# A two-block transformer kernel: the second block's attentions by pairs of heads

## The reference, cut to what matters

```python
for layer in range(2):
    u = rms_norm_2(h, norm_g[layer]) * (1 + scale) + shift
    uc = rms_norm_2(hc, norm_g[layer]) * (1 + scale_c) + shift_c
    y, yc = ab_mixer(u, uc, ...) if layer == 0 else c_mixer(u, uc, ...)
    h = h + gate * y            # hc likewise, but not after the last layer
return rms_norm_2(h, final_g)
```

## Time and profile before

| what | us |
|---|---|
| median of 3 runs | 1394.5 |
| lowest and highest | 1389.78, 1398.46 |
| the profiled execution | 1398.49 |
| its span, first to last instruction | 1396.7 |
| PE, DVE, ACT, POOL busy in it | 1267.5, 480.2, 430.7, 213.6 |
| mean granted TensorE clock | 0.963 |

### The profile page before, as it was taken

How to read it: one execution, slowest core, us unless ns; L and a number is a source line. 1 busy time by engine, 2 the same in 40 slices (tenths; PEclk the granted TensorE clock), 3 DMA queues, 4 the chain that set the end, 5 groups by cost and what they waited for, 6 DMA issues and landing times.

```text
span 1396.7 us, 17822 instructions
## 1 busy us (share of the span) xinstructions
PE 1267.5 (91%) x6740; PEld 805.5 (58%) x6740; DVE 480.2 (34%) x1128; ACT 430.7 (31%) x874; POOL 213.6 (15%) x374
## 2 busy tenths in 40 slices
PE   7997999798999999998989999989959899998996
PEld 6875665557533233334344233258848686987985
DVE  3564233443310002122222021133345435356544
ACT  4543333323220001133231001023325343545662
POOL 3004364100010000012010000014302123000320
PEclk9998887899999999999999999999979999999999
DMA  9546387343479999999999999965411203664200
GB/s 365 183 146 224 98 295 241 121 151 118 155 278 409 409 409 409 381 410 409 409 405 407 406 407 398 409 241 180 141 45 46 76 18 107 208 189 145 60 16 31
DMA packets 97037, 333.64 MB, mean 239 GB/s; under 512 B 10416, under 2 KB 10672, under 8 KB 96816
## 3 DMA queue, kind: packets, MB, share of 16 engines
q1 hardware_dynamic: 96944, 332.41, 64.4%
HBM read 331.32 MB, written 1.05 MB: 238 GB/s over the span
## 4 chain that ended last, share of the span: by engine, by line
PE 69%; DMA 16%; DVE 7%; ACT 3%; issue 2%; SPq 1%; POOL 1%; DVEq 0%; POOLq 0%; ACTq 0%
PE ps L453 23%; PE ps L505 8%; DMA w<-in_w_gate 7%; PE ps L1601 6%; DMA w<-in_w_up 6%; PE ps L2142 5%; PE ps L618 5%; PE ps L2185 3%; DMA w<-in_w_down 3%; PE ps L629 3%; PE ps L758 2%; PE ps L537 2%; PE ps L1168 2%; PE ps L1620 2%; PE ps L2161 1%
## 5 line engine op out<-in xcount | busy, mean ns | idle before, releaser
L2142 PE MATMUL ps<-w,vT 128*32 128x512 f32 x1024 | 196.0, 601 | 14.8 <-DMA w<-in_w_gate 8.0
L437 ACT ACTIVATE ab<-w 128x1024 fp32r<-128x1024 f32 (+2 forms) x117 | 121.9, 1048 | 209.4 <-PE ps L453 185.6
L447 DVE TENSOR_TENSOR ab<-w,ab 128x1024 fp32r<-128x1024 f32 (+2 forms) x96 | 117.9, 1234 | 187.7 <-ACT ab L437 187.6
L453 PE MATMUL ps<-ab,UA 128*128 128x512 f32 (+1 forms) x416 | 127.2, 387 | 6.2 <-DVE UB L1207 5.0
L2142 PEld LDWEIGHTS ps<-w,vT 128*32 128x32 f32 x1024 | 37.8, 108 | 152.9 <-issue 64.2
L453 PE MATMUL ps<-ab,uA 128*128 128x512 f32 x320 | 107.7, 419 | 10.7 <-POOL ab L447 4.2
L1601 PE MATMUL ps<-w,Uc 128*128 128x512 f32 (+1 forms) x224 | 102.8, 606 | 1.8 <-DVE Uc L1744 1.8
L453 PEld LDWEIGHTS ps<-ab,UA 128*128 128x128 f32 x416 | 77.7, 188 | 21.6 <-issue 5.3
L2185 PE MATMUL ps<-w,bT 128*32 128x512 f32 x512 | 78.8, 598 | 9.6 <-ACT bT L2238 5.5
L453 PE MATMUL ps<-ab,UB 128*128 128x512 f32 (+1 forms) x208 | 80.4, 386 | 0.0
L453 PEld LDWEIGHTS ps<-ab,uA 128*128 128x128 f32 x320 | 63.5, 202 | 27.5 <-POOL ab L447 4.7
(11 more groups left out here) (493 smaller groups left out, 2023.7 us busy)
## 6 DMA issues: line engine op xcount, KB each, us to landing
w<-in_w_gate SPq DMA_DIRECT2D x128, 512.0 KB, 10.9
w<-in_w_up SPq DMA_DIRECT2D x128, 512.0 KB, 11.7
w<-in_w_down SPq DMA_DIRECT2D x128, 512.0 KB, 11.8
w<-in_w_ada SPq DMA_DIRECT2D x48, 512.0 KB, 6.6
w<-in_w_c SPq DMA_DIRECT2D x48, 512.0 KB, 4.6
w<-in_w_m SPq DMA_DIRECT2D x16, 512.0 KB, 4.8
w<-in_ab_out_w SPq DMA_DIRECT2D x16, 512.0 KB, 7.9
w<-in_w_out SPq DMA_DIRECT2D x8, 512.0 KB, 5.8
```

What stands on the lines that cost most here:

```text
L437: e.activation(sp.a(j), w.v, ACT.Copy).then_inc(sp.whole, 1)
L447: e.tensor_tensor(sp.b(j), w.v, sp.a(j).bitcast(F32), ALU.subtract).then_inc(sp.parts[j % NAB], 1)
L453: ins = e.matmul(out_, l[x], r[y], start=start and n == 0, stop=stop and n == 2)
L2142: ins = e.matmul(t.ps[o, :], ve[:, p % 2, 2 * c + k, o], w.v[:, k, :], start=c + k == 0, stop=c + k == 4)
```

## The change

- WIN, LAT and NEAR become `Pairs`: two neighbouring heads and one query block at a time, 8, 8 and 16 of them. Scores of head 0 use rows 0 to 63 of PE, of head 1 rows 64 to 127, alternating (`halves`; LAT has 96 rows and does not); nothing is zeroed. Queries are scaled by minus 0.125 (or minus 96 to the -0.5), masks have the other sign, and DVE takes the minimum of mask plus scores over all 512 keys in one operation. The output product has the values as stationary operand, 64 columns for each head, so that it comes turned, [features, 128 queries]; two more products spread the reciprocals over it. DVE multiplies both into ZT, which is laid out turned. Transposes follow one step after the scores, outputs two.
- za, zb, c6 and c7 are made turned (`pe_linT`); bo and co are read in the row order "(k p)". The 16 transposes go; ACT and POOL or DVE split ZT in four parts, c = 0 to 3, some of them during the attention, and `pe_out_lin` waits part by part.
- The bias is built by POOL, per pair, into Bm, one pair ahead.
- Norms: the rows are scaled by ACT (row 1) and DVE (row 0) and transposed. For norm1 the mean square comes from the rows times gain before the first block's final norm is applied to h; that norm is moved behind norm1. The gain's row is made in the context's work, ahead of c5.
- The rotations come behind zb.3's split, ACT's splits of bo0 behind WIN; context c3 is run in two halves around the first transposes.

```diff
-        ZO = h[:, 2:4, :]
+        ZT = h[:, 2:4, :].rearrange("p i n -> p (i n)").rearrange("p (k t) -> p k t", k=8)
...
+        def pe_pairs(e, at, need=()):
+            for s, v in need:
+                e.wait_ge(s, v)
+            turned = {}
+            for step in range(at.n + 2):
+                if step < at.n:
+                    pr = at.pairs[step]
+                    ts = [bank.take(ALL, at.tag + "_s") for _ in range(2)]
+                    for t in ts:
+                        free(e, t)
+                    order = [(x, hp) for x in range(len(pr["k"])) for hp in range(2)]
+                    if not at.halves:
+                        order.sort(key=lambda o: o[1])
+                    for x, hp in order:
+                        c, n, k = pr["k"][x]
+                        ins = e.matmul(ts[hp].ps[:, c:c + n], pr["q"][hp], k[hp], start=True, stop=True)
+                        if x == len(pr["k"]) - 1:
+                            ins.then_inc(ts[hp].full, 1)
+                yield
+                p = step - 1
+                if 0 <= p < at.n:
+                    turned[p] = []
+                    for hp in range(2):
+                        t = bank.take(ALL, at.tag + "_t")
+                        free(e, t)
+                        e.wait_ge(*at.prob(2 * p + hp))
+                        for c in range(4):
+                            ins = e.transpose(t.ps[:, c * 128:c * 128 + 128], bP[:, (2 * p + hp) % 3, c * 128:c * 128 + 128], ident)
+                        ins.then_inc(t.full, 1)
+                        turned[p].append(t)
+                yield
+                p = step - 2
+                if p >= 0:
+                    pr, t, m = at.pairs[p], bank.take(ALL, at.tag + "_o"), st[:, p % 4, :]
+                    free(e, t)
+                    e.wait_ge(pair_rec, at.rec0 + p + 1)
+                    for hp in range(2):
+                        o = slice(64 * hp, 64 * hp + 64)
+                        e.matmul(t.ps[o, 128:256], m[:, 4 + hp:5 + hp].to_broadcast([128, 64]), ident, start=True, stop=True)
+                    for x in turned.pop(p):
+                        e.wait_ge(x.evac, x.n)
+                    for c in range(4):
+                        for hp in range(2):
+                            o = slice(64 * hp, 64 * hp + 64)
+                            ins = e.matmul(t.ps[o, 0:128], pr["v"][c][hp], bT[:, (2 * p + hp) % 3, c * 128:c * 128 + 128], start=c == 0, stop=c == 3)
+                    ins.then_inc(t.full, 1)
+                yield
+
+        def dve_pairs(e, at, ready=None):
+            for step in range(at.n + 3):
+                p = step - 3
+                if p >= 0:
+                    t, z = bank[at.tag + "_o"][p], at.pairs[p]["z"]
+                    e.wait_ge(t.full, t.n)
+                    chain(e.tensor_tensor(z, t.ps[:, 128:256], z, ALU.mult))
+                    e.tensor_tensor(z, t.ps[:, 0:128], z, ALU.mult).then_inc(t.evac, 1)
+                yield
+                if step < at.n:
+                    pr, m = at.pairs[step], st[:, step % 4, :]
+                    if ready:
+                        ready(step)
+                    for hp in range(2):
+                        u = 2 * step + hp
+                        t = bank[at.tag + "_s"][u]
+                        e.wait_ge(t.full, t.n)
+                        if at.masked:
+                            if u >= 2:
+                                e.wait_ge(*at.prob(u - 2))
+                            e.tensor_tensor_reduce(bS[:, hp, :], t.ps[:, :], pr["mask"][hp], 1.0, pr["nsink"][hp] if at.sink else 3e38,
+                                                   ALU.add, ALU.min, m[:, hp:hp + 1]).then_inc(t.evac, 1)
+                        else:
+                            e.tensor_reduce(m[:, hp:hp + 1], t.ps[:, :], X, ALU.min).then_inc(pair_top, 1)
+                yield
+                yield
+
+        def act_pairs(e, at, more=None):
+
+            for step in range(at.n + 1):
+                if step < at.n:
+                    m = st[:, step % 4, :]
+                    for hp in range(2):
+                        u = 2 * step + hp
+                        t = bank[at.tag + "_s"][u]
+                        e.wait_ge(*at.top(u))
+                        if u >= 3:
+                            g = bank[at.tag + "_t"][u - 3]
+                            e.wait_ge(g.full, g.n)
+                        src = bS[:, hp, :] if at.masked else t.ps[:, :]
+                        ins = e.activation(bP[:, u % 3, :], src, ACT.Exp, bias=m[:, hp:hp + 1], scale=-1.0, accum_out=m[:, 2 + hp:3 + hp])
+                        ins.then_inc(pair_prob if at.masked else t.evac, 1)
+                if step > 0:
+                    for hp in range(2):
+                        u = 2 * step - 2 + hp
+                        t = bank[at.tag + "_t"][u]
+                        if u >= 3:
+                            g = bank[at.tag + "_o"][(u - 3) // 2]
+                            e.wait_ge(g.full, g.n)
+                        e.wait_ge(t.full, t.n)
+                        e.activation(bT[:, u % 3, :], t.ps[:, :], ACT.Copy).then_inc(t.evac, 1)
+                if at.sink and step < at.n:
+                    e.wait_ge(sink_away, step + 1)
+                    e.activation(m[:, 6:8], m[:, 6:8], ACT.Exp).then_inc(sink_exp, 1)
+                if more:
+                    more(step)
+
+        def pool_pairs(e, at, before_=None):
+            for step in range(at.n):
+                m = st[:, step % 4, :]
+                if before_:
+                    before_(step)
+                if at.sink:
+                    e.wait_ge(*at.top(2 * step))
+                    e.wait_ge(*at.top(2 * step + 1))
+                    e.tensor_tensor(m[:, 6:8], m[:, 0:2], at.pairs[step]["sink"], ALU.add).then_inc(sink_away, 1)
+                e.wait_ge(*at.prob(2 * step))
+                e.wait_ge(*at.prob(2 * step + 1))
+                if at.sink:
+                    e.wait_ge(sink_exp, step + 1)
+                    G_.did(e.tensor_tensor(m[:, 2:4], m[:, 2:4], m[:, 6:8], ALU.add))
+                    G_.after()
+                e.tensor_tensor(m[:, 4:6], m[:, 2:4], C("minus").to_broadcast([128, 2]), ALU.pow).then_inc(pair_rec, 1)
+
+
+        o_upper, o_lower, o_lower_v = sem("o_upper"), sem("o_lower"), sem("o_lower_v")
...
+        def out_lower(e, zT, c, n, done):
+
+            e.wait_ge(o_upper, n)
+            e.tensor_tensor(UB[:, 2 * c:2 * c + 2, :], zT[:, 2 * c:2 * c + 2, :], UA[:, 2 * c:2 * c + 2, :].bitcast(F32), ALU.subtract).then_inc(done, 1)
...
+        def pe_rows_to_T(e, name, n):
+
+            for i in range(2):
+                pe_to_T(e, name, lambda k: scaled_rows[i].rearrange("p (d k) -> p k d", k=8)[:, k, :], 8, ALL,
+                        (diag_ready, 2 + n) if i == 0 else (rows_act, n))
...
-            pe_row_bcast(e, "grown", lambda k: S("gfin")[:, k:k + 1], ALL)
-            some(later, 3)
-            for i in range(2):
-                pe_norm(e, "norm1", i, diag(i), (diag_ready, 3 + i), ALL)
-            some(later, 1)
+            some(later, 2)
+            pe_rows_to_T(e, "norm1", 1)
+            some(later, 2)
...
-            pe_lin(e, S2, "za", UA, UB, 512, range(2), (1, 3))
-            pe_lin(e, S2, "zb", UA, UB, 512, range(2), (1, 3))
-            some(later, 4)
-            for i in range(2):
+            pe_linT(e, S2, "za", UA, UB, (1, 3))
+            pe_linT(e, S2, "zb", UA, UB, (1, 3))
+            for i in range(2):
+                some(later, 2)
                 pe_to_T(e, "qaT", lambda k: qa[:, i, k * 128:(k + 1) * 128], 4, ALL, (kd_ready2, i + 1))
                 pe_to_T(e, "kaT", lambda k: kd[:, k, :, :].rearrange("p a r -> p (a r)"), 2, ALL)
             for i in range(2):
                 pe_to_T(e, "cqT", lambda k: cq[:, i, 0:384].rearrange("p (d k) -> p k d", k=3)[:, k, :], 3, ALL)
                 pe_to_T(e, "ckT", lambda k: ck[:, i, :].rearrange("p (d k) -> p k d", k=2)[:, k, :], 2, ALL)
-            beside(pe_attend(e, WIN, ALL, [(kaT_zero, 2), emptied("kaT")] + [emptied("qaT", i) for i in range(2)]), pe_queries(e))
+            beside(pe_pairs(e, WIN, [emptied("kaT")] + [emptied("qaT", i) for i in range(2)]), pe_queries(e))
...
-            for _ in pe_attend(e, LAT, ALL, []):
+            for _ in pe_pairs(e, LAT):
                 pass
-            e.wait_ge(*emptied("lat_o"))
-            for i in range(2):
-                pe_to_T(e, "mT", lambda k: ZO[:, i, :].rearrange("p (d k) -> p k d", k=8)[:, k, :], 8, ALL)
-            all_emptied(e, "mT")
-            for c in range(2):
-                pe_lin(e, S2, f"bo{c}", UA, UB, 512, range(2), (1, 3))
-
-            some(later, 3)
-            for i in range(2):
-                pe_norm(e, "norm2", i, diag(i), (diag_ready, 5 + i), ALL)
-            some(later, 1)
+            pe_out_lin(e, "bo", [(o_lower, 1), (o_lower, 2), (o_lower_v, 1), (o_lower_v, 2)], (1, 3))
+
+            some(later, 2)
```

(45 more changed lines are left out.)

270 lines of the change are left out of this document (143 added, 127 removed).

## The result

| | before | changed | forecast |
|---|---|---|---|
| median, us | 1392.45 (4 runs) | 1325.05 (4 runs) | 1324 |
| lowest and highest | 1389.78, 1398.46 | 1322.26, 1330.13 | 1303 to 1352 |
| profiled execution | 1398.49 | 1322.26 | |
| mean granted clock | 0.963 | 0.973 | |

The ratio is 0.951 (95% interval 0.947 to 0.956): 67 us less. The forecast took 70.4 off a median of three runs, 1394.5; the fourth run of before moved its median to 1392.45. The two profiled executions lie 76.2 apart, since that of before was the slowest of its four and that of the changed kernel the fastest of its four.

What follows compares the result with a forecast made beforehand. PE was taken as the bound, over 85% busy in five of eight windows. Stage savings summed to 70.4 us: 1328 from the profiled 1398.5, 1324 for the median (before: 1394.5); range 1303 to 1352.

Steps and rivals of the forecast that it cites:

- Rotations no longer behind bo0: From zb's end to the first window scores: rotations end before PE needs them, 16.6 for 33.6 us, saved 17.0.
- Rival 3: The hole at 1006 us stays, held by another late landing or c3: 13 us back, 1337; chance 0.08.
- Pairs: Window and near attention: two heads side by side in array halves take 3.23 us a pair for 4.40.
- change of form: Switch between whole-array and half-array products on PE: 0.11 us each, three a window or near pair, bounds 0 and 0.15.
- Rival 2: Array halves run one after the other in the attentions: 57 us back, 1381; chance 0.12, in part or whole.
- latent pair: Latent attention, whose 96 rows can't be halved: 4.04 us a pair including two changes; stage saved 2.7 us.
- Rival 1: A pair is held by ACT or by issue at about 4.0 us: price 18 us, 1342; chance 0.15.
- Window attention: Window stage by pairs, with PE's idle time falling: 37.5 us for 49.0, saved 11.5.
- norm1: Second block's first norm, rows scaled on ACT and DVE: first product at +20.6 us instead of +26.0, saved 5.4.
- norm2: Second block's later norm, scaled rows transposed: +18.3 us instead of +22.4, saved 4.1.
- Turned products, seams: za, zb, c6, c7 made turned lose 2.8 us; seams behind the attentions, without 16 transposes each, save 4.7 and 5.0.
- Rival 4: Half-array work in the attentions is granted only 1.2 GHz: 110 us more, 1434; chance 0.05.

Runs made afterwards that it cites:

- the two runs on the order: Changed kernel with bo0's splits back ahead of the rotations and context c3 whole ahead of the first transposes: 1339.6 us; with only c3 whole: 1329.0 us.
- outputs by head: Changed kernel with the output products of all 32 pairs ordered head 0, then head 1, instead of alternating: 1349.5 us.
- the run with the diagonal: Changed kernel with norm2 done as before, TensorE multiplying by the diagonal of the roots instead of transposing scaled rows: 1333.1 us.
- scores by head: Changed kernel with the scores of window and near pairs ordered head 0, then head 1, instead of alternating: 1325.5 us.
- outputs in twos: Changed kernel with each pair's output products taken two of head 0, two of head 1 and so on, instead of alternating: 1330.6 us.

## Why the prediction was right, and where it was off

**The total** (1324 for 1325.05) is the sum of steps that each were near; the largest stage error is 1.9 us. That it agrees to 1 us is partly luck all the same: the saving was forecast at 70.4 and measured at 67.4 by medians, and the median of before came out 2 lower than the one that the forecast started from. By profiles the second block gave 68.6 for 70.4, and 7.6 more lie in the experts' stage, for which the forecast had nothing.

**Rotations no longer behind bo0**: 17.0 for 17.1, and by the two runs on the order the cause is the one read from the earlier trace rows. Rival 3 is out.

**Pairs**: 3.23 for 3.33. The halves run side by side: without halved rows a pair takes 0.71 more, and the outputs of both heads take 0.27 + 0.97 = 1.24 up to the next scores, for the 1.10 of one head's ten records and a change of form, where the two heads one after the other would take 2.20. Rival 2 is out. No run put the outputs in whole-array form; the 0.70 of the outputs by head is the price of an order in which halves overlap in part. The term that was small is the change of form: I took 0.11, by the earlier trace rows it could be up to 0.15, and the run with two more of them measured 0.15. Three of them are 0.12 more a pair. A second term was slightly large, the pace of the scores. The changed kernel's latent scores, in whole-array form and with no change between, are 0.43 apart, two records each:

```profile
1065.60 0.59 PE L787 MATMUL ps<-kbTc,qbT 96*128 96x256 f32 x2
1066.03 0.59 PE L787 MATMUL ps<-kbTx,qbT 96*128 96x256 f32 x2
```

At that pace four records take 0.87, not 0.92; what is left over in a pair of 3.33, beside 0.88 and 1.10, is then 0.48 for three changes, 0.16 each. A latent pair took 4.04, just as forecast, because there both errors, in eight records and two changes, cancel: that agreement is luck. What was wrong in the step is its reason: "since the two heads now alternate in program order". For scores the order did not matter at all; it matters for outputs, where five products stand in a row.

**Rival 1** (ACT or issue at 4.0) is out: no idle time stands in a pair, and ACT is busy 45.0 of 56.7.

**Window attention**: 38.1 for 37.5. Its last pairs, with no queries between them, stand 3.33 apart.

**norm1** was the weak step: 3.5 for 5.4. The chain was counted from the experts' end, 925.4, as if DVE began there. In the changed kernel it began 4.7 us behind that end, by an issue wait, for which the chain had no term. In the kernel before, PE was busy 23.4 of that stage's 26.0, and DVE's first instruction there waited for PE; its diagonals were ready at 937.6, 1.5 us before PE took them:

```profile
928.80 2.04 DVE L2651 COPY bP<-ps 128x512 f32<-128x512 f32 x2 [3.45 <-PE ps L1579]
937.12 0.48 DVE L2658 TENSOR_SCALAR bP<-cst,rs 128x128 f32<-128x128 f32 x2 [1.64 <-POOL rs L588]
939.07 7.67 PE L537 MATMUL ps<-bP,h 128*128 128x128 f32 x32
```

So a late start of some microseconds could hide there behind PE; whether DVE's issue was late in that kernel too, its one profile does not show. The chain itself, 17.8 from DVE's first product, was shorter than the 20.6 forecast. The blocks took 8.5 where I counted 9.5, and row 0 was ready 7.5 after DVE's start and row 1 8.0, where I had +9. Both errors together leave 1.9.

**norm2**: 4.8 for 4.1, and the run with the diagonal gives back just these 4.8.

**Turned products, seams**: within 0.3 and 0.

**Rival 4** (the clock falls): not by half-array work itself; behind the first pairs of near attention the clock is 1.00 in the profiles. But behind the stop of 1.25 or 2.7 us ahead of an attention it falls in some executions, at a cost of 1.2 to 2.9 us. The prediction said "here no stop is left"; two short ones are, one of them the start of near attention for which its own sum kept PE's wait.

**Still open**: of the 7.6 us in the experts' stage, 5.6 is the spread of that stage over profiles of one code path. There is one profile of the kernel before, and by medians the gain (67.4) is already covered by the second block (68.6). I didn't test whether anything of the change reaches into the experts' stage. Nor did a run take back the products made turned, the bias on POOL, norm1's scaled rows or the outputs that arrive turned; for these only the stages of one profile before and one after stand against the forecast.

## What to carry to other kernels

When you take work from the engine that bounds a stage, ask at once what that work covered, and count the next chain from where its first engine really starts: here DVE started 4.7 us behind the stage's border. When two heads fit into halves of TensorE's array, put their products in turn or in twos, count 0.15 us for each change of form, and check that no other engine exceeds the new pair. Moving POOL's split out of a chain that runs over DVE and POOL gained 0.2 of 1.9 us here, since the split then ran beside a DVE instruction of that chain.

## What the runs showed of the hardware that I had not expected

- TensorE started a product of a free half while two earlier products of the busy half were unfinished, not more (scores by head: no loss; outputs in twos: 0.05 us a pair; five in a row: start 0.71 late, with two left).
- A DVE scaling of 128x1024 took 2.42 us beside a POOL split of 1.94, in both runs that put them side by side, and 0.75 with no split beside it.
- After the same PE stops of 2.7 and 1.25 us the granted clock fell to 0.50 in some executions (five of ten, three of thirteen) and stayed at 1.00 in the others; the fall cost 1.2 to 2.9 us.
- A change between whole-array and half-array products cost about 0.15 us (two more of them a pair: 0.30 us on 3.33 and on 4.04).
- Where the experts' stage ends, DVE's next instruction was issued 3.0 to 6.1 us late, differently in each execution.
